# Index of the samples in strips of two with early gathers, far bias among the second group's query tiles

## What is computed

```python
# indexer, prompt and samples
dots = einsum('bqhd,bkd->bqhk', q_idx, k_idx)
score = einsum('bqhk,bqh->bqk', relu(dots), w_idx) * IDX_SCALE
sel = top_k(score, 256)          # of 2049 keys for a sample; 128 of 512 for a prompt query
# attention over the selected keys, with a relative bias
bias = rel_bias[t5_bucket(q_pos - sel)]      # 32 buckets x 8 heads
p = softmax(q @ k_sel / 8 + bias);  o = p @ v_sel
```

## Time and profile before

| | us |
|---|---|
| median of 3 runs | 1165.07 (1163.37 to 1166.27) |
| profiled execution | 1163.57 |
| its span, first to last instruction | 1161.8 |
| TensorE busy | 1125.1 (97%) |
| VectorE busy | 686.5 (59%) |
| ScalarE busy | 398.9 (34%) |
| GpSimd busy | 101.6 (9%) |
| mean granted clock of TensorE | 0.987 |

### The profile page before, as it was taken

One profiled execution on the slowest core, in us unless ns is written; L12 is line 12 of the kernel. 1 busy time (PEld: TensorE's weight loads), 2 busy tenths in 40 slices (PEclk: granted clock), 3 DMA queues, 4 the chain that ended last, 5 costly groups with the idle time before them and its releaser, 6 DMA issues.

```text
span 1161.8 us, 22104 instructions
## 1 busy us (share of the span) xinstructions
PE 1125.1 (97%) x9038; PEld 983.1 (85%) x9038; DVE 686.5 (59%) x1541; ACT 398.9 (34%) x758; POOL 101.6 (9%) x155
## 2 busy tenths in 40 slices
PE   7999999898998999999999999899999999999998
PEld 5898886465575899999989777589999999999998
DVE  4545844979787587778886634545454545453440
ACT  4522323622577755555555424521011101000000
POOL 3100002001106300000000111100000000000000
PEclk9999999978999999999999999999999999999999
DMA  9997651022011202222213377513333333252341
GB/s 322 270 279 183 197 147 55 1 73 82 28 32 52 82 2 82 83 83 83 83 32 114 138 254 254 212 44 91 90 90 91 92 92 93 73 141 76 100 121 28
DMA packets 141874, 129.15 MB, mean 111 GB/s; under 512 B 17635, under 2 KB 135824, under 8 KB 139712
## 3 DMA queue, kind: packets, MB, share of 16 engines
q1 hardware_dynamic: 137184, 86.78, 25.4%
q0 software_dynamic: 4608, 41.23, 9.7%
HBM read 124.58 MB, written 3.41 MB: 110 GB/s over the span
## 4 chain that ended last, share of the span: by engine, by line
PE 85%; DVE 7%; ACT 3%; issue 2%; DMA 2%; POOL 0%; ACTq 0%; DVEq 0%; POOLq 0%
PE psV L1290 22%; PE psV L1033 15%; PE psA L1290 11%; PE psA L673 9%; PE psV L1158 4%; PE psV L946 3%; PE psA L1013 2%; PE psV L705 2%; PE psV L804 2%; PE psA L1083 2%; PE psV L969 1%; PE psA L955 1%; DMA r<-cache_idx,rows_of 1%; PE psV L714 1%; PE psA L1123 1%
## 5 line engine op out<-in xcount | busy, mean ns | idle before, releaser
L1033 PE MATMUL psV<-r_r,wide_r 128*128 128x260 f32 x1536 | 207.7, 288 | 2.8 <-DVE msk L2243 2.2
L1033 PEld LDWEIGHTS psV<-r_r,wide_r 128*128 128x128 f32 x1536 | 190.4, 189 | 5.3 <-issue 3.5
L1586 ACT ACTIVATE wring<-psV 128x512 f32<-128x512 f32 x128 | 76.3, 597 | 92.9 <-PE psV L1033 70.5
L1290 PE MATMUL psV<-qiz_r,wring_r 128*128 128x260 f32 x528 | 93.9, 283 | 0.0
L2444 DVE TENSOR_TENSOR wide<-wide,psV 128x520 f32<-128x520 f32 x22 | 15.3, 697 | 126.6 <-PE psV L1290 126.6
L2244 DVE TENSOR_REDUCE msk<-wring 128x8 f32<-128x512 f32 x128 | 86.4, 676 | 0.0
L1290 PEld LDWEIGHTS psV<-qiz_r,wring_r 128*128 128x128 f32 x528 | 76.2, 188 | 0.0
L673 PE MATMUL psA<-wide_r,wring_r 128*128 128x260 f32 x416 | 76.0, 285 | 0.0
L1290 PE MATMUL psA<-qiz_r,wring_r 128*128 128x260 f32 x352 | 70.9, 283 | 0.0
L1290 PE MATMUL psA<-qiz_r,r_r 128*128 128x260 f32 x352 | 70.9, 282 | 0.0
L1290 PE MATMUL psA<-hT_r,r_r 128*128 128x260 f32 x352 | 70.8, 283 | 0.0
(11 more groups left out here) (568 smaller groups left out, 2504.9 us busy)
## 6 DMA issues: line engine op xcount, KB each, us to landing
wring<-w_ffn_in SPq DMA_DIRECT2D x44, 512.0 KB, 3.7
wide<-w_ada SPq DMA_DIRECT2D x11, 1024.0 KB, 7.4
wring<-w_ffn_out SPq DMA_DIRECT2D x16, 704.0 KB, 4.6
tok<-w_ada SPq DMA_DIRECT2D x9, 1024.0 KB, 5.4
wring<-w_in SPq DMA_DIRECT2D x24, 256.0 KB, 5.9
wring<-w_out SPq DMA_DIRECT2D x8, 512.0 KB, 5.8
wide<-w_out SPq DMA_DIRECT2D x2, 2048.0 KB, 7.9
r<-w_ada SPq DMA_DIRECT2D x3, 1024.0 KB, 10.7
```

Of the source, the lines that this page charges most:

```text
L1033: mm = pe.matmul(kx[m % 2][:, hf, :], w, wtab[:, b % 2, l, 2 * k + hf, :], start=(k == 0 and w is high and l == 0), stop=(k == 1 and w is ...
L1290: mm = pe.matmul(out[:, hf, 0:HT], w[:, k, :], x[:, hf * HT:(hf + 1) * HT], start=(k0 + k == 0 and x is xh and w is high), stop=(k0 + k == ...
L1586: A(sq2[m % 2].rearrange("p (x n) -> p x n", x=2), kx[m % 2][:, :, 0:256], ACT.Square).then_inc(kx_squared, 1)
```

## The change

The far bias leaves the small products and is made in two parts in the second group, at p = 20 and p = 21, in the PSUM tile `o_by_pair(4)`; `rbias` moves to another place in SBUF. The index takes whole samples: seven slots of 4 KB per partition, four of them in `qiz`, in-place copies of 1024 columns, and products with 32 columns of weights into strips of 32 partitions, for two samples in different strips at a time. `w1` and the new token's index products are made before the first rounds. The rounds are spread anew: 6, 12 and 11 before the relu, the rest at tiles 1, 3, ..., 33, 41, 44 and 47. `copy_group` goes from VectorE to ScalarE. Row numbers for the gathers are made early. Semaphore counts follow.

```diff
+        hflat_rb = hT[:].rearrange("p a t -> p (a t)")[0:32, 2100:2108]
-        ip = r1[:, 3848:5896].rearrange("p (s n) -> p s n", s=2)
-        kiT = r1[:, 0:1024].rearrange("p (s n) -> p s n", s=2)
+        idx_flat = qiz[:].rearrange("p a t -> p (a t)")
+        idx_slots = [r1[:, 3848:4872], r1[:, 4872:5896]] + [idx_flat[:, x * 1024:(x + 1) * 1024] for x in range(4)] + [r1[:, 0:1024]]
+        IDX_ORDER = (0, 2, 1, 3, 4, 6, 5, 7)
+        IDX_SETS = {2: (0, 1), 4: (2, 3), 6: (4, 5), 7: (6, 7)}
...
 # TensorE
-            pe.wait_ge(v_free, V_FAR - 1)
-            for j in range(NPG + 1):
-                cols = ohf[:, j:PAST:NPG] if j < NPG else ohf[:, PAST:PAST + 1].broadcast_to([NBUCK, 128])
-                mm = pe.matmul(sv(V_FAR)[:, 0, j * 8:(j + 1) * 8], cols, rbias, start=True, stop=True, skip_group_check=True)
-            mm.then_inc(v_full, 1)
...
-            pe.wait_ge(queries_ready, 1)
+            pe.wait_ge(queries_ready, 5)
...
+            def idx_products(at):
+                pe.wait_ge(a_free, A_IP + max(at) + 1)
+                for g in range(2):
+                    for x in at:
+                        b = IDX_ORDER[x]
+                        r = slice(32 * (b // 2), 32 * (b // 2) + 32)
+                        mm = pe.matmul(sv(V_IS)[r, g, :], w1[:, b * 128:(b + 1) * 128][:, r], idx_slots[x % 7][:, g * 512:(g + 1) * 512],
+                                       start=(b % 2 == 0), stop=(b % 2 == 1), skip_group_check=True)
+                return mm
+            for x in range(NB):
+                pe.wait_ge(pages_in[x % 7], 16 * (x // 7 + 1))
+                pe.wait_ge(a_free, A_IP + x - 1)
+                for y in range(8):
+                    mm = pe.transpose(out[:, y * 128:(y + 1) * 128], idx_slots[x % 7][:, y * 128:(y + 1) * 128], ident)
+                mm.then_inc(a_full, 1)
+                if x in IDX_SETS:
+                    mm = idx_products(IDX_SETS[x])
...
+            def far_bias(at):
+                pe.wait_ge(o_free, 4)
+                for j in at:
+                    cols = ohf[:, j:PAST:NPG] if j < NPG else ohf[:, PAST:PAST + 1].broadcast_to([NBUCK, 128])
+                    mm = pe.matmul(o_by_pair(4)[:, j * 8:(j + 1) * 8], cols, rbias, start=True, stop=True, skip_group_check=True)
+                return mm
...
                 if 0 <= p < NP:
                     turn_pair(p)
+                if p == 20:
+                    far_bias(range(0, 9))
+                if p == 21:
+                    far_bias(range(9, NPG + 1)).then_inc(o_turned, 1)
...
 # ScalarE
-            A(far, sv(V_FAR)[:, 0, 0:136].rearrange("p (j h) -> p j h", h=8), ACT.Identity).then_inc(v_free, 1)
...
+                A(idx_slots[x % 7], sa(A_IP + x).rearrange("p b n -> p (b n)"), ACT.Identity).then_inc(a_free, 1)
...
+                if u >= 13 and u % 8 == 5 and u < NA:
+                    copy_group(act, u // 8 - 1)
...
             latent_high(act, 0)
+            copy_group(act, 7)
...
 # VectorE
-            ROUND_AT = list(range(1, 20, 2))
+            ROUND_AT = list(range(1, 34, 2)) + [41, 44, 47]
             v.wait_ge(v_full, V_BIAS + 1)
             v.tensor_scalar(g8, sv(V_BIAS)[0:8, 0, 0:384], -1.0, None, ALU.mult).then_inc(v_free, 1)
-            for _ in range(8):
+            link(v.memset(w1, 0.0))
+            w1v = w1.rearrange("p (b x) -> p b x", x=144)
+            for p0, c in ((0, 0), (64, 8)):
+                for odd in range(2):
+                    v.tensor_copy(w1v[p0:p0 + 64, :, c + odd:c + 8:2],
+                                  qiz[odd * 64:odd * 64 + 64, odd:8:2, SEQ:T].rearrange("p h b -> p b h")).then_inc(queries_ready, 1)
+            v.tensor_tensor(irel[:, 0:64].rearrange("p (h b) -> p h b", h=H), qiz[:, :, SEQ:T],
+                            kidxT[:, SEQ:T].unsqueeze(1).broadcast_to([128, H, NB]), ALU.mult).then_inc(new_ready, 1)
+            for _ in range(6):
                 next(rounds)
...
-            for _ in range(15):
+            for _ in range(12):
                 next(rounds)
...
-            for _ in range(16):
+            for _ in range(11):
                 next(rounds)
...
-                if u >= 13 and u % 8 == 5:
-                    copy_group(u // 8 - 1)
...
+                if u == 45:
+                    v.wait_ge(o_turned, 5)
+                    v.tensor_copy(far, o_by_pair(4)[:, 0:136].rearrange("p (j h) -> p j h", h=8)).then_inc(o_free, 1)
...
 # GpSimd
-            for b in range(NB):
-                if b >= 2:
-                    g.wait_ge(a_full, A_IP + 2 * b - 2)
-                fetch(ip[:, b % 2, :], "cache_idx", IDX, b, pages_in[b % 2])
+            for x in range(NB):
+                if x == 2:
+                    g.wait_ge(queries_ready, 4)
+                    g.wait_ge(new_ready, 1)
+                if x == 7:
+                    g.wait_ge(a_full, A_IP + 4)
+                fetch(idx_slots[x % 7], "cache_idx", IDX, IDX_ORDER[x], pages_in[x % 7])
```

More of the change, by code:

```diff
@@ L428, in build @@
         mask_ready, top_done = sem("mask_ready"), sem("top_done")
-        pages_in = [sem(f"pages_in{x}") for x in range(2)]
-        IDX_IN = 16 * NB // 2
-        kv_rows = [sem(f"kv_rows{x}") for x in range(3)]
+        pages_in = [sem(f"pages_in{x}") for x in range(7)]
+        IDX_IN = (32, 16)
         lat_turned, lat_high, lat_split, kx_full, kx_squared, kx_dotted, page_sums, ss_ready = (sem(x) for x in (
@@ L904, in pe_program @@
             pe.wait_ge(queries_ready, 6)
[L906 to L924, removed]
+            def idx_products(at):
[7 more added lines that the diff above has]
+                return mm
+            pe.wait_ge(v_free, V_IS - 1)
+            for x in range(NB):
+                pe.wait_ge(pages_in[x % 7], 16 * (x // 7 + 1))
+                pe.wait_ge(a_free, A_IP + x - 1)
+                out = sa(A_IP + x).rearrange("p b n -> p (b n)")
+                for y in range(8):
[3 more added lines that the diff above has]
+                    mm = idx_products(IDX_SETS[x])
             mm.then_inc(v_full, 1)
@@ L1528, in act_program @@
             A(ssnew[:], ssnew[:], ACT.Sqrt, scale=1.0 / NOPE, bias=epsc[0:NB]).then_inc(ssn_root, 1)
-            for n in range(16):
-                act.wait_ge(a_full, A_IP + n + 1)
-                A(kiT[:, n % 2, :], sa(A_IP + n)[:, 0, :], ACT.Identity).then_inc(a_free, 1)
+            for x in range(NB):
+                act.wait_ge(a_full, A_IP + x + 1)
+                A(idx_slots[x % 7], sa(A_IP + x).rearrange("p b n -> p (b n)"), ACT.Identity).then_inc(a_free, 1)
             for u in range(NA + 2):
@@ L1924, in dve_program @@
             v.wait_ge(tab_loaded, 160)
+            v.tensor_scalar(rows_of[:], ptab[:], 8.0, sel[:, 80:81], ALU.mult, ALU.add).then_inc(rows_ready, 1)
             link(v.tensor_tensor(cosg, cosg, grow.unsqueeze(1).broadcast_to([128, 5, ROPE]), ALU.mult))
@@ L2023, in dve_program @@
             ins.then_inc(qrope_done, 1)
-            v.wait_ge(tab_loaded, 160)
-            v.tensor_scalar(rows_of[:], ptab[:], 8.0, sel[:, 80:81], ALU.mult, ALU.add).then_inc(rows_ready, 1)
-            link(v.memset(w1, 0.0))
             v.wait_ge(norm_done, len(normed))
             v.tensor_scalar(qcat[0:64, :, SEQ:T], qcat[0:64, :, SEQ:T], gT[0:64, G_KN:G_KN + 1], None, ALU.mult).then_inc(queries_ready, 1)
-            w1v = w1.rearrange("p (b x) -> p b x", x=144)
-            for p0, c in ((0, 0), (64, 8)):
-                for odd in range(2):
-                    v.tensor_copy(w1v[p0:p0 + 64, :, c + odd:c + 8:2],
-                                  qiz[odd * 64:odd * 64 + 64, odd:8:2, SEQ:T].rearrange("p h b -> p b h")).then_inc(queries_ready, 1)
             v.tensor_copy(qd[:].rearrange("p (b h) -> p b h", b=NB), qz[:, :, SEQ:T].rearrange("p h b -> p b h")).then_inc(queries_ready, 1)
-            for _ in range(15):
+            for _ in range(12):
                 next(rounds)
@@ L2045, in dve_program @@
             v.tensor_scalar(wz[:], sel[:, 0:64], small[:, 8:9], None, ALU.mult).then_inc(new_ready, 1)
-            v.tensor_tensor(irel[:, 0:64].rearrange("p (h b) -> p h b", h=H), qiz[:, :, SEQ:T],
-                            kidxT[:, SEQ:T].unsqueeze(1).broadcast_to([128, H, NB]), ALU.mult).then_inc(new_ready, 1)
             v.wait_ge(v_full, V_WC + 2)
@@ L2507, in pool_program @@
             g.wait_ge(v_free, V_BIAS + 1)
-            for b in range(NB):
-                if b >= 2:
-                    g.wait_ge(a_full, A_IP + 2 * b - 2)
-                fetch(ip[:, b % 2, :], "cache_idx", IDX, b, pages_in[b % 2])
+            for x in range(NB):
+                if x == 2:
[4 more added lines that the diff above has]
+                fetch(idx_slots[x % 7], "cache_idx", IDX, IDX_ORDER[x], pages_in[x % 7])
             mla_rows = lambda b: fetch(pgs[:, b % 2].rearrange("p j n -> p (j n)"), "cache_mla", ROW, b, pages_in[b % 2])
-            kv_rows_of = lambda b, s: fetch(kvp[s].rearrange("p j n -> p (j n)"), "cache_kv", 256, b, kv_rows[s])
```

(1 more changed line is left out.)

37 lines of the change are left out of this document (17 added, 20 removed).

## The result

The changed kernel took 1179.72 us (median of 4 runs, 1178.56 to 1181.23), the kernel before on the same chip 1165.67 (4 runs, 1163.37 to 1172.5): a ratio of 1.0106, 95% interval 1.0069 to 1.0142. It is slower by 12 us by that ratio (the two medians lie 14 us apart); the forecast was 1166.6 with a range up to 1172.5. The profiled execution took 1178.74, its span is 1176.9, and the mean granted clock fell from 0.987 to 0.966.

The account below looks back on a forecast made before the run. Bound by TensorE and VectorE nearly tied, then the index chain, then TensorE in the attention. Terms -14.7 + 1.0 + 8.2 + 6.0 + 0.5 + 0.5 = +1.5 us gave 1166.6 us, range 1162.5 to 1170.5 (overall 1159.5 to 1172.5).

Parts of the forecast that it names:

- the rounds moved into the attention: Tiles 19 to 34: VectorE becomes the bound, 22.1 us instead of 13.90, +8.2 (bounds +8.0 to +10.5).
- the scaling's new wait: Behind the toeplitz products: TensorE waits 2.8 us for VectorE's scaling of the samples' queries once the far bias is gone.
- the price of a far instruction: Second group, far bias: each instruction costs its weight load, 0.218 us, the same at either clock.
- rival C: Index products: strips do not overlap, products stay at 13.8 us, L2074 6.0 later, 1172.6 in all; chance 0.08.
- The copies on ScalarE: Attention: copies of a group's output moved to ScalarE cost +0.5 us (0 to +1.5).
- the relu: End of the index: L2074 starts at 285.1 us, not 299.83, -14.7, before +1.0 for the early gathers.
- the late table: Toeplitz load: early gathers share its queues, so L859 and all behind it come +1.0 us later (0 to +2.5).
- the copy of the new keys: Ahead of the index: copied at 265.45 instead of 270.15 us, 4.7 earlier, before the +1.0 for the gathers.
- the term of the clock: Second group, p = 22 and 23: lower clock left by the far bias's thin matmuls costs +0.5 us (0 to +2.5).
- the 6.0: Second group, p = 20 and 21: far-bias matmuls less TensorE's waits cost +3.4 and +2.6 us (bounds +4.5 to +7.5).
- the rounds at tiles 41, 44 and 47: Second group: rounds at tiles 41 and 44 lie under the far bias and cost nothing.
- rival B: Attention: clock falls in tiles 19 to 33, +4.7 us, and +2.5 behind the far bias, 1173.8 in all; chance 0.20.

Follow-up runs that it names:

- y3: Changed kernel with the far bias back behind the toeplitz products and the rounds placed as in the kernel before; 1174.87 us, ratio 1.0082.
- z1: Changed kernel with far bias back, gathers 2 to 7 held for the toeplitz table, rounds respread (9/16/9, fifteen in attention); 1161.11 us, ratio 0.9954.
- z4: y3 with 38 extra 128x128 products between the last strip product and the first tile's product; 1171.8 us, ratio 1.0037.
- y1: Changed kernel with the index gathers of samples 2 to 7 held until the toeplitz table has landed; 1175.45 us, ratio 1.0077.
- x2: Changed kernel without the last ten top-k rounds of the prompt's last query tile; 1164.34 us, ratio 0.998.
- x3: Changed kernel with only one of seventeen far-bias blocks made, at p = 21; 1170.0 us, ratio 1.0018.
- x1: Changed kernel with the far bias alone put back behind the toeplitz table; 1174.07 us, ratio 1.0061.
- x4: Changed kernel with extra unread 128x128 products, eight a pair at p = 9 to 19 and four at p = 20 to 23; 1190.99 us, ratio 1.0196.
- z2: x1 with three extra 128x128 products a pair from tile 18 to 47, 45 in all; 1171.02 us, ratio 1.0027.
- z3: y3 with seventy extra 128x128 products between the last strip product and the first tile's product; 1178.75 us, ratio 1.0086.
- y2: x1 with the rounds put into VectorE's waits: 10/17/11 ahead of the relu, eleven in the attention; 1167.99 us, ratio 1.0009.

## Why the prediction was wrong

- *Right:* the rounds moved into the attention, +8.2 foretold, +8.0 measured, with VectorE nearly without gaps (20.70 of 21.88 us); the scaling's new wait, 2.88 for 2.8; the price of a far instruction, 0.22 us at either clock; strips that overlap (rival C is dead). The copies on ScalarE were priced at 0.5 and cost somewhat more: TensorE waits 0.62 us for one (hT, L1573) in the last tiles, where 0.8 was lost, and tiles 34 to 40 and 46 to 48 take 5.8 and 2.9 in place of 5.5 and 2.7 even at the full clock (y3, z1, z4).
- *Half right:* the relu, -13.7 foretold with the late table, -11.2 behind g8 measured. What is missing stands ahead of the copy of the new keys, which came 1.0 us earlier behind g8 (33.3 for 34.3) where 3.7 was foretold. L861 began 2.8 later than L859 had (1.0 foretold), 1.6 of it by the collision of gathers and table (y1), and L883 took 6.99 us where L886 took 5.14, at a lower clock. Since the same code takes 4.26 to 6.99 us there, that part is not shown to be the change's.
- *The step that failed is the term of the clock.* The forecast had the path wrong there, and not only the size: it read "The thin matmuls of the far bias leave a lower clock behind ... At p = 22 and 23 that costs +0.5 (0 to +2.5)", and it came only behind the far bias. Measured: 2.2 us ahead of the far bias (tiles 34 to 40), 3.4 above the 6.0 in tiles 40 to 46 and 2.1 in 46 to 48, together 7.7. Of these 0.6 are lost at the full clock too (see the copies above), and at most 1.3 are what the rounds at tiles 41, 44 and 47 cost under the far bias, which the forecast put at nothing (tiles 40 to 48: 21.7 with them, 20.4 in x2 without); the rest, 5.8 to 7.1, is the clock, 0.50 where it was 1.00. Tiles 0 to 16 took 1.6 more, at a lower clock as well, but x3 with the same code up to there took 28.5, as before, so this is not shown to be the change's. x2 shows that the far bias lowers the clock by itself (4.2 us), x3 and x1 that VectorE's rounds do so by themselves, x4 and z2 that extra products in TensorE's waits prevent it. That is rival B's mechanism, with a chance of 0.20. It came later than B put it, since the clock went down only at 336 us, when tiles 19 to 33 were half done, and VectorE's 21.9 us hid it there. That B's 7.2 is close to the 7.7 is luck: 4.7 of it were to come in tiles 19 to 33, where nothing was lost, and 2.5 behind them.
- Sum: 1.5 foretold, +7.2 in tiles 34 to 48 (7.7 less the 0.5), +1.6 in tiles 0 to 16, +2.5 at the relu make 12.8, against 12.4 above the kernel before by the ratio and 12.0 from g8 to tile 48 by the two profiles. The profiled pair has 2.6 us more ahead of g8, which is scatter; how much of the 1.6 and the 2.5 is scatter too stays open.
- *The trace of before had the warning.* The far bias stood in it with TensorE busy 4.00 of 4.00 us and the granted clock falling to 0.65. The forecast carried that over as a small cost of two pairs. But there toeplitz products of full width stand ahead of it, and the clock was back at about 260 us, 7 us later. Against B stood "1.00 at 13.32 of 13.90 busy"; after the change TensorE is busy 2.67 of 4, a state which that row doesn't speak of. The Trainium skill ("TensorE: Matmul & The Clock Gate", Part 4: PE-mode transpose) says that transposes don't count as busy for the clock gate. The pairs of tiles 19 to 47 are in good part transposes; no run here took these out, so whether they count was not tested.

Open: how the 6.3 us of the rounds in x3 divide between the clock and the rounds at tiles 41 and 44, for z2 took 9.2 in tiles 40 to 46 at the full clock where before took 7.5; why tiles 0 to 16 took 30.1 in x1 and 26.8 in z2, which are the same up to there (TensorE waited 0.9 us for the relu in x1 and 0.3 in z2, which may be the cause; nothing here set that wait by itself); and what about the work in tiles 19 to 47 decides whether the clock falls, since z3 and y2 had dips there and z2 none.

## What to carry to other kernels

An engine freed early is no gain in itself: if it then waits for another, its clock can fall and the next wide products pay (y3: 9.25 us of wait, then 4 us lost against before). Move work so that the two engines arrive together, and put the lighter engine's rounds beside the widest products (z1), not beside the small ones. Once down, the clock stayed down long: in the changed kernel, x2, x3 and y1 up to about the first scores of 384 columns, whichever of the two causes had lowered it. When a stretch changes from TensorE-bound to bound by another engine, price everything behind it at the lower clock as well; and look at what narrow products did to the clock where they stand now, before they are moved in among others.

## What the hardware showed that was not expected

- An instruction of 8 columns with 32 rows of weights takes 0.22 us at either clock (18 in 4.07 us, most of them at 1.00, in x2; 18 in 4.06 at 0.50 in the changed kernel), while TensorE shows as fully busy, and the granted clock falls to 0.50 all the same (x2, x4).
- An extra fp32 product of 128x128 is two instructions in the trace and costs 0.22 to 0.28 us (70 in 15.9 us, three in 0.83), about twice a transpose of the same size, which is one (eight in a row: 1.04 us).
- Two column strips at once take 1.91 us for eight instructions of 512 columns, four strips 1.06; one after the other eight take 3.44, at 0.86 for two (L909, kernel before). That is 1.8 and 3.2 times as fast.
- The start of a run isn't fixed: g8 stood from 234.5 to 242.0 us behind the first instruction in twelve profiles of the same code ahead of it, with a granted clock of the first 40 us between 0.79 and 0.96. The time to the relu and that of the first tiles scatter by some us as well, so one profile of each kernel can't settle a difference of 1 or 2 us that stands ahead of an edit.
